# Compressed branch of a sparse-attention layer: block columns as the stationary operand, the inner width on two partition halves, the keys' chain apart from the values' chain

## The reference, cut to what matters

```python
    def compress(tok, pe, w1, w2):
        blocks = tok[:, blk_idx] + pe[None, None, :, None, :]
        flat = blocks.transpose(0, 1, 3, 2, 4).reshape(bsz, n_cmp, G, CMP_LEN * HD)
        return (jax.nn.gelu(flat @ w1) @ w2).transpose(0, 2, 1, 3)

    kc = compress(kc_tok, pe_k, w1_k, w2_k)
    vc = compress(vc_tok, pe_v, w1_v, w2_v)
    ...
        p_c = masked_softmax(jnp.einsum('bghqd,bgcd->bghqc', qb, kc),
                             cmp_end[None, :] <= t[:, None])
        o_c = jnp.einsum('bghqc,bgcd->bghqd', p_c.astype(vc.dtype), vc)
    ...
        return gb[..., 0:1] * o_c + gb[..., 1:2] * o_s + gb[..., 2:3] * o_w
```

## Time and profile before

| what | us |
|---|---|
| median of 3 runs | 1250.45 |
| lowest, highest run | 1250.06, 1256.01 |
| profiled execution | 1251.81 |
| its span, first to last instruction | 1250.0 |
| TensorE busy in it | 1208.8 (97%) |
| GpSimd busy | 674.1 (54%) |
| VectorE busy | 629.4 (50%) |
| ScalarE busy | 317.1 (25%) |

### The profile page before, as it was taken

One profiled execution on the slowest core, in us unless ns is written; L12 is line 12 of the kernel. 1 busy time (PEld: TensorE's weight loads), 2 busy tenths in 40 slices (PEclk: granted clock), 3 DMA queues, 4 the chain that ended last, 5 costly groups with the idle time before them and its releaser, 6 DMA issues.

```text
span 1250.0 us, 18894 instructions
## 1 busy us (share of the span) xinstructions
PE 1208.8 (97%) x6854; PEld 997.1 (80%) x6854; DVE 629.4 (50%) x1212; ACT 317.1 (25%) x664; POOL 674.1 (54%) x610
## 2 busy tenths in 40 slices
PE   7999999998998999999999999999999999999997
PEld 6777778777887877877888888877888888888885
DVE  3885554388824575544566666663354300334122
ACT  3125121124631324212015444420221100112001
POOL 4884444334536586755323433456566666666663
PEclk9999999997999999999789999999999999999999
DMA  7222110114013232234321111112232333233321
GB/s 243 85 84 68 45 60 34 52 51 119 1 35 105 71 87 82 85 95 146 124 67 52 51 52 52 51 56 97 84 101 85 100 101 101 85 100 101 118 85 68
DMA packets 29684, 102.41 MB, mean 82 GB/s; under 512 B 3632, under 2 KB 6064, under 8 KB 28848
## 3 DMA queue, kind: packets, MB, share of 16 engines
q1 hardware_dynamic: 27232, 93.47, 23.9%
q10 hardware_dynamic: 2384, 7.99, 2.0%
...
...
## 4 chain that ended last, share of the span: by engine, by line
PE 85%; DVE 7%; POOL 3%; issue 2%; ACT 2%; DMA 1%; SPq 0%; DVEq 0%; POOLq 0%; ACTq 0%
PE acc L277 23%; PE acc L278 21%; PE acc L279 21%; PE aux L488 3%; POOL w_lo L1517 3%; PE aux L1573 2%; PE aux L784 2%; PE aux L478 2%; PE aux L1557 1%; PE aux L852 1%; PE aux L344 1%; PE aux L853 1%; PE acc L488 1%; DMA residual<-x 1%; DVE conv_sum L1884 1%
## 5 line engine op out<-in xcount | busy, mean ns | idle before, releaser
L1509 POOL CAST w_hi<-w_raw 128x1024 fp32r<-128x1024 f32 x164 | 177.5, 1083 | 524.1 <-issue 375.7
L1517 POOL TENSOR_TENSOR w_lo<-w_raw,w_hi 128x256 fp32r<-128x256 f32 x352 | 288.2, 849 | 7.1
L277 PE MATMUL acc<-ht_hi,w_hi 128*128 128x512 f32 x672 | 273.9, 408 | 4.3 <-DVE ht_lo L388 2.3
L279 PE MATMUL acc<-ht_hi,w_lo 128*128 128x512 f32 x672 | 265.0, 394 | 0.0
L278 PE MATMUL acc<-ht_lo,w_hi 128*128 128x512 f32 x672 | 264.8, 394 | 0.0
L1512 POOL TENSOR_TENSOR w_lo<-w_raw,w_hi 128x1024 fp32r<-128x1024 f32 x76 | 188.3, 2478 | 6.1
L277 PEld LDWEIGHTS acc<-ht_hi,w_hi 128*128 128x128 f32 x672 | 128.1, 191 | 34.9 <-POOL w_lo L1517 3.7
L279 PEld LDWEIGHTS acc<-ht_hi,w_lo 128*128 128x128 f32 x672 | 127.7, 190 | 27.8
L278 PEld LDWEIGHTS acc<-ht_lo,w_hi 128*128 128x128 f32 x672 | 128.2, 191 | 24.6 <-issue 1.2
L277 PE MATMUL acc<-w_hi,ht_hi 128*128 128x512 f32 x256 | 106.8, 417 | 0.3
L277 PE MATMUL acc<-w_hi,ff_hi 128*128 128x512 f32 x256 | 99.7, 390 | 2.3 <-POOL w_lo L1512 2.3
...
## 6 DMA issues: line engine op xcount, KB each, us to landing
...
```

The costliest lines, as they stand in the source:

```text
L277: nc.tensor.matmul(bank, ah, bh, start=start, stop=False)
L279: return nc.tensor.matmul(bank, al, bh, start=False, stop=stop)
L1509: nc.gpsimd.tensor_copy(w_hi[:, slot], raw[:, j]).then_inc(hi_split, 1)
L1517: done = nc.gpsimd.tensor_tensor(w_lo[:, slot, kk, cols], raw[:, j, kk, cols], w_hi[:, slot, kk, cols].bitcast(F32), ALU.subtract)
```

## The change

On TensorE the roles in the hidden product are swapped. The stationary operand is now a strip of 63 block columns (both groups with the column between them, which nobody reads), the moving one 128 columns of `cmp_w1`. The two halves of the inner width go to partitions 0 to 62 and 64 to 126 of one bank (`hid_rows`; `aux2` for keys, `aux1` for values) and alternate matmul by matmul. The result has blocks on partitions, so ScalarE copies it to `hraw`, TensorE transposes it (`hidden_flip`) into the second quarter of the same bank, and the gelu reads it there. A dummy gelu loads ScalarE's table ahead.

The order changes too. Twelve pieces instead of ten stand ahead of the keys' products. Behind them come one piece, the transpose, two pieces, then the flips of the first branch's output, and the values' products right behind these. The keys' second product signals `cmp_kv` by itself; VectorE scales all four gate banks, copies the keys and signals `cmp_z`; the scores start without the values. The values' second product comes behind the scores, and VectorE copies the values (`values_four_times`) between the two halves of the softmax. The second gate slab has 1 + 7 + 1 pieces ahead of the attention instead of 2 + 5, and the attention skips the piece in every 7th step instead of every 9th.

```diff
+        hraw = [sb("cmp_hidden_rows_k", [P, P], F32, 198), sb("cmp_hidden_rows_v", [P, P], F32, 204)]
+        hid_rows = [slice(hh * DH, hh * DH + 2 * CMP_C - 1) for hh in range(2)]
+        hid_bank = [aux[2], aux[1]]
...
-        GATES_AHEAD, SPARED = 7, 9
+        GATES_AHEAD, SPARED = 9, 7
...
-            fill(10)
-
-            for kv in range(2):
-                pe.wait_ge(on["cmp_blocks"], kv + 1)
-                if kv:
-                    pe.wait_ge(on["rot_used"], N_ROPED + 1)
+            fill(12)
+
+            def hidden_products(kv):
                 for ab in range(2):
                     pe.wait_ge(w1_in[ab], 16 * (kv + 1))
-                    for hh in range(2):
-                        for lp in range(8):
-                            bank = aux[2 * (1 - kv) + hh]
-                            o = bank[:, 0:2 * CMP_C].rearrange("p (g c) -> p g c", g=2)[:, :, 0:N_CMP]
-                            done = nc.tensor.matmul(o, w1[:, ab, lp, hh * P:(hh + 1) * P],
-                                                    xc[:, kv, ab, lp, :, ab:ab + N_CMP],
+                    for lp in range(8):
+                        for hh in range(2):
+                            done = nc.tensor.matmul(hid_bank[kv][hid_rows[hh], 0:P],
+                                                    xc[:, kv, ab, lp].rearrange("p g c -> p (g c)")
+                                                    [:, ab:ab + 2 * CMP_C - 1],
+                                                    w1[:, ab, lp, hh * P:(hh + 1) * P],
                                                     start=ab == 0 and lp == 0, stop=ab == 1 and lp == 7)
                     done.then_inc(w1_used, 1)
-                if kv == 0:
-                    fill(4)
-
-                    pe.wait_ge(on["ya_ready"], 1)
-                    pe.wait_ge(on["hid_out"], 1)
-                    flip_on_tensor(pe, lambda t, k: AG[:, t, k * P:(k + 1) * P], 4, FLIP_A)
-                    fill(1)
-                    pe.wait_ge(flip_lo, FLIP_A + 2)
-            pe.wait_ge(flip_lo, FLIP_A + 4)
+
+            def hidden_flip(kv):
+                pe.wait_ge(on["hid_out"], 2 * kv + 1)
+                nc.tensor.transpose(hid_bank[kv][:, P:2 * P], hraw[kv][:], ident).then_inc(w1_used, 1)
+
+            pe.wait_ge(on["cmp_blocks"], 1)
+            hidden_products(0)
+            fill(1)
+            hidden_flip(0)
+            fill(2)
+            pe.wait_ge(on["ya_ready"], 1)
+            pe.wait_ge(on["hid_out"], 2)
+            flip_on_tensor(pe, lambda t, k: AG[:, t, k * P:(k + 1) * P], 4, FLIP_A)
+            pe.wait_ge(on["cmp_blocks"], 2)
+            pe.wait_ge(on["rot_used"], N_ROPED + 1)
+            pe.wait_ge(flip_lo, FLIP_A + 2)
+            hidden_products(1)
+            pe.wait_ge(flip_lo, FLIP_A + 3)
             pe.wait_ge(w2_in, 16)
             for hh in range(2):
                 done = nc.tensor.matmul(aux[2][:, 0:2 * CMP_C], w2[:, 0, hh], hid[:, 0, hh], start=hh == 0,
                                         stop=hh == 1)
+            done.then_inc(on["cmp_kv"], 1)
             gates = [slab_in_pieces(pe, U_GATE + UPS * n, ht_hi, ht_lo, SLAB_GATE + n, False)
                      for n in range(1, GATE_SLABS)]
-            gates[0](2)
+            gates[0](1)
+            hidden_flip(1)
+            pe.wait_ge(flip_lo, FLIP_A + 4)
+
+            pe.wait_ge(on["cmp_z"], 1)
+            for t in range(NT):
+                for c in range(4):
+                    if t == 2 and c == 0:
+                        pe.wait_ge(on["hid_out"], 4)
+                    o = aux[t // 2][:].rearrange("p (t g c k) -> p t c g k", t=2, g=2, c=4)[:, t % 2, c]
+                    done = nc.tensor.matmul(o, PB2[:, 8 + c, t * P:(t + 1) * P], kcz[:], start=True, stop=True)
+                if t % 2:
+                    done.then_inc(on["c_scores"], 1)
             pe.wait_ge(on["hid4_ready"], 1)
             for g in range(2):
                 for hh in range(2):
                     done = nc.tensor.matmul(aux[3][:, g * DH:(g + 1) * DH], hid4[:, hh, g], w2[:, 1, hh, 0:DH],
                                             start=hh == 0, stop=hh == 1)
             done.then_inc(on["cmp_kv"], 1)
-
-            pe.wait_ge(on["cmp_z"], 1)
-            for t in range(NT):
-                for c in range(4):
-                    o = aux[t // 2][:].rearrange("p (t g c k) -> p t c g k", t=2, g=2, c=4)[:, t % 2, c]
-                    done = nc.tensor.matmul(o, PB2[:, 8 + c, t * P:(t + 1) * P], kcz[:], start=True, stop=True)
-                if t % 2:
-                    done.then_inc(on["c_scores"], 1)
             gates[0](GATES_AHEAD - 2)
             for a in range(2):
                 pe.wait_ge(on["c_probs"], a + 1)
+                if a:
+                    gates[0](1)
+                    pe.wait_ge(on["cmp_z"], 2)
...
+            nc.scalar.activation(small(364, 1), rstd[:, 0:1], ACT.Gelu_apprx_tanh, scale=0.0)
...
-                    act.wait_ge(w1_used, 4)
+                    act.wait_ge(w1_used, 5)
                 act.wait_ge(on["hid_zero"], 1)
+                nc.scalar.activation(hraw[kv][:], hid_bank[kv][:, 0:P], ACT.Copy).then_inc(on["hid_out"], 1)
+                act.wait_ge(w1_used, 3 * kv + 3)
                 for hh in range(2):
+                    first = P + hh * DH
                     done = nc.scalar.activation(
                         hid[:, kv, hh, :, 0:N_CMP],
-                        aux[2 * (1 - kv) + hh][:, 0:2 * CMP_C].rearrange("p (g c) -> p g c", g=2)[:, :, 0:N_CMP],
+                        hid_bank[kv][:, first:first + DH].rearrange("p (g c) -> p g c", g=2)[:, :, 0:N_CMP],
...
-            eng.wait_ge(w1_used, 3)
-            for b in range(2):
+            eng.wait_ge(w1_used, 4)
+            for b in range(4):
                 scale_gate(0, b, gate_a, 0)
-            eng.wait_ge(on["hid_out"], 2)
+            eng.wait_ge(on["cmp_kv"], 1)
+            for g in range(2):
+                rows = slice(g * DH, (g + 1) * DH)
+                done = V.tensor_copy(kcz[rows, g], aux[2][rows, g * CMP_C:(g + 1) * CMP_C])
+                if g == 0:
+                    step(done)
+            done.then_inc(on["cmp_z"], 1)
+            eng.wait_ge(on["gate_th"], 1)
+            step(V.tensor_scalar(sg[:], sg[:], 0.5, 0.5, ALU.mult, ALU.add))
+            eng.wait_ge(on["hid_out"], 4)
             for hh in range(2):
                 done = V.tensor_copy(hid4[:, hh], hid[:, 1, hh].unsqueeze(2).to_broadcast([P, 2, 4, CMP_C]))
                 if hh == 0:
                     step(done)
             done.then_inc(on["hid4_ready"], 1)
-            eng.wait_ge(on["gate_th"], 1)
-            step(V.tensor_scalar(sg[:], sg[:], 0.5, 0.5, ALU.mult, ALU.add))
-            eng.wait_ge(on["cmp_kv"], 1)
-            for g in range(2):
-                rows = slice(g * DH, (g + 1) * DH)
-                step(V.tensor_copy(kcz[rows, g], aux[2][rows, g * CMP_C:(g + 1) * CMP_C]))
-            for h in range(4):
-                rows = slice(h * CMP_C, (h + 1) * CMP_C)
-                done = V.tensor_copy(vcz[rows, :, h], aux[3][rows, 0:2 * DH].rearrange("p (g d) -> p g d", g=2))
-                if h < 3:
-                    step(done)
-            done.then_inc(on["cmp_z"], 1)
-            for b in range(2, 4):
-                scale_gate(0, b, gate_a, 0)
+
+            def values_four_times():
+                eng.wait_ge(on["cmp_kv"], 2)
+                for h in range(4):
+                    rows = slice(h * CMP_C, (h + 1) * CMP_C)
+                    done = V.tensor_copy(vcz[rows, :, h], aux[3][rows, 0:2 * DH].rearrange("p (g d) -> p g d", g=2))
+                    if h < 3:
+                        step(done)
+                done.then_inc(on["cmp_z"], 1)
...
+                if a == 0:
+                    values_four_times()
```

## The result

The changed kernel takes 1235.4 us (median; 1233.6 to 1236.6), the kernel before in the same runs 1252.0. The medians differ by 16.6 us; the ratio is 0.986, 95% interval 0.984 to 0.988, so 1.4% less. The forecast was 1233, its range 1228 to 1241. The time is inside the range and the change has the sign that was forecast; several steps of the walk to it came out otherwise, and some of these errors cancelled.

The account below looks back on a forecast made before the run. TensorE's work plus waits bound it (85% of the span). 61.19 - 44.0 - 1.7 = 15.5 us, with -2.72 and +0.7 in the attention 17.5: 1251.81 to 1234.3, 1.4 lower for the median: 1233, range 1228 to 1241.

Parts of the forecast that it names:

- the walk: TensorE's steps and waits at full clock, from the eleventh gate piece's end at 600.37 us to the attention: 44.0 us.
- The products: Hidden products of keys and values: column halves overlap, so each takes 32 x 0.111 = 3.55 us; bounds 1.9 and 7.1.
- Rival A: Hidden products: the column halves don't overlap, 1238 us, or 1245 with load and stream in series; chance 0.12.
- D: Hidden products: each change of half drains the array, 17.3 us per product, slower at 1258 us; chance 0.03.
- The wait for `w_lo`: Ahead of the thirteenth gate piece, TensorE waits 2.0 us for GpSimd's last step on the next weight unit.
- The wait for `ya_ready`: Ahead of the first branch's flips, TensorE waits 2.4 us for VectorE, slowed beside GpSimd; bounds 0 and 4.
- Each delays the other by about its own work: Price of VectorE and GpSimd running side by side ahead of the first flips: `ya_ready` moves by 2.9 us.
- The clock: One fall between 612.9 and 618.1 us, around the 16 transposes: 3.41 us at half speed, cost 1.7; bounds 0 and 6.5.
- rival B: Clock low for longer, from 603.6 us or from 617 to the pieces behind the scores: 1236 to 1240; chance 0.10.
- The waits behind: After the first flips: 1.1 us for `ya_lo`, none ahead of the scores, scores 3.55 us instead of 6.38.
- The second probabilities: Ahead of the attention: VectorE has them ready at about 640, where TensorE comes at 639.8, so even.
- The attention: Two gate pieces fewer inside it, -2.72 us, and uncovered waits for `probs`, +0.7.

Follow-up runs that it names:

- One half alone: Changed kernel with the hidden products of the upper column half left out except the first and last (36 passes per product, not 64); 1237.7 us, one run.
- the old form's second: Second trace of the changed kernel with the hidden products in their old form (128 columns loaded, 62 streamed); profiled execution 1255.6 us, median 1244.6.
- the chains joined: Changed kernel with the values' second product and the values' copy put back ahead of the scores, TensorE waiting for both copies; 1242.1 us, ratio 0.991.
- two pieces less: Changed kernel with seven instead of nine second-slab gate pieces ahead of the attention, and every ninth attention step without a piece, not every seventh; 1240.5 us.

## Why the prediction was right, and where it was not

**The products: right, for the reason given.** 32 x 0.111 = 3.55 us forecast, 3.65 measured from the first to what follows, 3.60 in the table of stretches. One half alone took the same. Rival A is out, and so is D: a change of half saves time (0.38 us each up to seven), it does not drain anything that shows. The rule of the Trainium skill that I had set against it (TensorE: Matmul & The Clock Gate, Part 3) would have a load wait for the matmuls in flight where the rows are the same. Here the loads of both halves are on the same rows; they were busy for 3.45 of 3.60 us beside matmuls busy for all of it, and the figure that would follow from load and stream in series, 10.8 us, did not come. This trace disagrees with that rule, and the kernel before already did: in the earlier trace rows the old products' loads, on all 128 rows, were busy for all of 7.09 us beside the matmuls.

**The wait for `w_lo`: right,** 1.87 for 2.0.

**The wait for `ya_ready`: wrong.** 2.4 us forecast, none measured. Two terms failed. VectorE's signal came 13.9 us behind the eleventh piece, not 14.9: the steps beside GpSimd cost 1.10 to 1.18 for 0.69, 1.7 us on four of them, and there are 0.7 more on the block columns, 2.4 together where I had 3.4. "Each delays the other by about its own work" priced it too high; GpSimd's cast and split took 6.4 us for 3.8 alone. And TensorE came 14.5 us behind it, not 12.5; 1.7 of these 2.0 are the low clock, which stood in front of this point.

**The clock: size right, place wrong.** One fall of 3.4 us was forecast, behind the 16 transposes. It came in front of the keys' products, behind the wait for `w_lo`, where rival B had put one. B's was to last through the keys' products and a piece, some 10 us; it lasted 3.4. From 612.95 to 619.80, transposes and wait included, the clock stayed at 1.00. Of the thirteen other traces only the old form's second has a fall behind this passage, at 631.98, 2.4 us into the values' products. The Trainium skill's rule that transposes don't count as TensorE being busy (same page, Part 4) made me surer of a fall there; the changed kernel's traces don't bear that out. Because I put the fall behind the wait for `ya_ready` and not ahead of it, I counted both, 1.7 and 2.4; where they stood they overlap, and only the fall is paid. TensorE was through with this place 2.1 us sooner than forecast, and 0.5 went again behind it: that is the 1.6 us by which the stretch was shorter than the 45.7 forecast.

**The waits behind: right.** `ya_lo` 1.19 for 1.1; none ahead of the scores; scores 3.52 at full clock for 3.55. With the chains joined 2.6 us of waits came back, and 5.1 of clock behind them. The walk priced this at 6.38 - 3.55 and 1.86, without saying that most of it was clock.

**The second probabilities: right by luck.** Even was forecast and even it was, by two errors that cancel. TensorE waits for them ahead of the piece, not ahead of the second flips where I had set its arrival. By my own walk that is 1.8 us sooner, 638.0, and VectorE's 640 would have meant a wait of 2 us. But VectorE needed 12.35 us from the first logits to the end (627.45 to 639.80), not 15.4: 1.1 of the difference is its wait for the scores at the low clock, which is gone, and 1.8 are the company of GpSimd, 1.0 us where I had 2.8 in the sum (0.8 of it inside the 12.1). TensorE takes the piece here:

```profile
639.91 0.47 PE L277 MATMUL acc<-ht_hi,w_hi 128*128 128x512 f32 x1
```

So the margin was 0.1 us, and with two pieces less TensorE waits for 2.37.

**The attention: right,** 2.1 us for 2.0.

**The time.** Stretch and attention brought 19.2 us, 1.7 more than forecast, and the profiled execution was only 15.2 shorter. The rest is outside: the thousand microseconds that the change doesn't touch were 1.8 us longer ahead of the stretch and 2.2 behind the attention. Two falls of the clock make up these 2.2. One is at the last flips: they take 3.48 us for 1.97 (the earlier trace rows show full clock there before), but TensorE then no longer waits 0.95 for `yb_lo`, and 0.6 is left. The other, 1.6, is behind the last wait for `w_lo`, which both kernels have (2.31 and 2.32 us):

```profile
820.82 0.49 PE L277 MATMUL acc<-yb_hi,w_hi 128*128 128x512 f32 x1 [0.95 <-DVE yb_lo L388]
...
1233.30 0.50 PE L277 MATMUL acc<-w_hi,ff_hi 128*128 128x512 f32 x1 [2.32 <-POOL w_lo L1512]
```

```profile
803.88 0.63 PE L277 MATMUL acc<-yb_hi,w_hi 128*128 128x512 f32 x1
...
1216.52 0.50 PE L277 MATMUL acc<-w_hi,ff_hi 128*128 128x512 f32 x1 [2.31 <-POOL w_lo L1539]
1217.20:1220.62 3.42, 3.42 (x10) 2.63 (x9) 0.75 (x1) 0.74 (x3) 0.00 (x0) 0.50 0.00 0
```

The first pair of rows is the kernel before, the second the changed one. Both traces of the changed kernel have both falls. Of the experiments two others have the one at the last flips, and eight others the one at the wait. Whether the change causes them stays open. 1233 was close through two errors of opposite sign: 1.7 us too little gain in stretch and attention, 4.0 us that I had not expected outside.
